# The gate projections of a hybrid attention trunk move out of the merge stage and wait in DRAM

## What is computed

```python
h = rms_norm(x, attn_norm_w[i])
proj = h @ w_in[i]
dq, dk, dv, cq, ckv, krope, xq, gates = jnp.split(proj, IN_SPLIT_POINTS, axis=-1)
...   # y_a: differential attention, 8 heads; y_b: latent attention (MLA), 8 heads; y_c: cross-attention, 4 heads
g_a, g_b, g_c = jnp.split(jax.nn.sigmoid(gates), N_BRANCHES, axis=-1)
x = x + (g_a * y_a + g_b * y_b + g_c * y_c) @ w_out[i]
h2 = rms_norm(x, ffn_norm_w[i])
f_gate, f_up = jnp.split(h2 @ w_gate_up[i], 2, axis=-1)
x = x + (jax.nn.silu(f_gate) * f_up) @ w_down[i]
```

## Time and profile before

| | |
|---|---|
| median of 3 runs | 2238.22 us (2237.4 to 2241.2) |
| profiled execution, its own time | 2232.99 us |
| its span, first to last instruction | 2231.2 us |
| granted TensorE clock, mean of the span | 0.959 (1 is 2.4 GHz) |
| PE busy | 2135.6 us (96%), 9581 matmuls |
| DVE, ACT, POOL busy | 1052.9, 867.8, 874.1 us |
| DMA | 191.29 MB, mean 86 GB/s |
| share of the chain that ended last | PE 79%, DVE 11%, ACT 6%, issue 4% |

### The profile page before, as it was taken

The page is one execution under the profiler, slowest core; times in us unless marked ns, Lnnn a source line. Parts: engine busy times, 40 slices in busy tenths (PEclk is TensorE's granted clock), DMA queues, the critical chain, the costliest instruction groups (busy, mean ns, idle before and its releaser), DMA issues.

```text
span 2231.2 us, 31130 instructions
## 1 busy us (share of the span) xinstructions
PE 2135.6 (96%) x9581; PEld 1712.5 (77%) x9581; DVE 1052.9 (47%) x1813; ACT 867.8 (39%) x1513; POOL 874.1 (39%) x402
## 2 busy tenths in 40 slices
PE   4999999989999999999989899999899999999998
PEld 3876777767888888888878677776688888888886
DVE  6458777773222433331144878777522234333212
ACT  4444545553222433223343454545522233322333
POOL 2433222213444354445643322222244444444564
PEclk7999989989999999999999999899799999999998
DMA  5322111113333333323343211112233333333333
GB/s 179 91 78 60 44 49 46 44 36 114 103 95 95 94 95 100 97 86 119 97 143 83 72 48 53 40 44 57 80 100 94 94 95 95 98 99 94 110 97 113
DMA packets 352101, 191.29 MB, mean 86 GB/s; under 512 B 22614, under 2 KB 348316, under 8 KB 351132
## 3 DMA queue, kind: packets, MB, share of 16 engines
q1 hardware_dynamic: 349582, 175.97, 27.6%
q10 hardware_dynamic: 2446, 14.44, 1.8%
HBM read 182.49 MB, written 7.86 MB: 85 GB/s over the span
## 4 chain that ended last, share of the span: by engine, by line
PE 79%; DVE 11%; ACT 6%; issue 4%; DVEq 0%; ACTq 0%; POOL 0%; POOLq 0%
PE proj L528 24%; PE proj L530 24%; PE proj L529 24%; DVE p_a L1244 3%; PE flip L578 2%; ACT p_a L879 2%; ACT k_hi_hi L858 1%; PE score L563 1%; DVE mid L1206 1%; DVE rot L1205 1%; DVE rot L1204 1%; PE att L511 1%; PE att L512 1%; PE att L510 1%; PE score L562 1%
## 5 line engine op out<-in xcount | busy, mean ns | idle before, releaser
L493 POOL TENSOR_TENSOR w_lo<-raw,w_hi 128x1024 fp32r<-128x1024 f32 x352 | 859.0, 2443 | 1336.4 <-ACT w_hi L858 1335.7
L528 PE MATMUL proj<-h_hi,w_hi 128*128 128x512 f32 (+1 forms) x1648 | 658.2, 399 | 5.9 <-ACT kvT L858 1.4
L530 PE MATMUL proj<-h_hi,w_lo 128*128 128x512 f32 (+1 forms) x1648 | 643.7, 391 | 0.0
L529 PE MATMUL proj<-h_lo,w_hi 128*128 128x512 f32 (+1 forms) x1648 | 643.6, 391 | 0.0
L858 ACT ACTIVATE w_hi<-raw 128x1024 fp32r<-128x1024 f32 x356 | 374.3, 1053 | 207.7 <-PE proj L530 79.7
L528 PEld LDWEIGHTS proj<-h_hi,w_hi 128*128 128x128 f32 (+1 forms) x1648 | 310.5, 188 | 79.0 <-issue 9.4
L529 PEld LDWEIGHTS proj<-h_lo,w_hi 128*128 128x128 f32 (+1 forms) x1648 | 310.6, 188 | 67.7 <-issue 4.4
L530 PEld LDWEIGHTS proj<-h_hi,w_lo 128*128 128x128 f32 (+1 forms) x1648 | 310.1, 188 | 66.0
L528 PE MATMUL proj<-hid_hi,w_hi 128*128 128x512 f32 x352 | 136.9, 389 | 0.0
L529 PE MATMUL proj<-hid_lo,w_hi 128*128 128x512 f32 x352 | 136.9, 389 | 0.0
L530 PE MATMUL proj<-hid_hi,w_lo 128*128 128x512 f32 x352 | 136.9, 389 | 0.0
(11 more groups left out here) (269 smaller groups left out, 3131.2 us busy)
## 6 DMA issues: line engine op xcount, KB each, us to landing
raw<-in_w_in SPq DMA_DIRECT2D x232, 256.0 KB, 3.0
raw<-in_w_gate_up SPq DMA_DIRECT2D x176, 256.0 KB, 3.0
raw<-in_w_down SPq DMA_DIRECT2D x96, 192.0 KB, 2.4
raw<-in_w_out SPq DMA_DIRECT2D x40, 256.0 KB, 2.8
raw<-in_w_mem_kv SPq DMA_DIRECT2D x32, 256.0 KB, 2.8
raw<-in_w_o_diff SPq DMA_DIRECT2D x32, 256.0 KB, 2.8
x_scratch<-xT ACTq DMA_DIRECT2D x2, 2048.0 KB, 9.1
raw<-in_w_o_mla SPq DMA_DIRECT2D x16, 256.0 KB, 2.7
```

Source lines behind the costliest of these rows:

```text
L493: g.tensor_tensor(w_lo[s][:, :], raw[s % 2][:, :], w_hi[s][:, :].bitcast(F32), ALU.subtract).then_inc(slot_lo.sem, 1)
L528: mm(o, hi[:, c:c + width], rh, start=start and k == 0, stop=False)
L529: mm(o, hi[:, c:c + width], rl, start=False, stop=False)
L530: ins = mm(o, lo[:, c:c + width], rh, start=False, stop=stop and k == n - 1)
```

## The change

- The 24 gate units of a layer leave stage E. Two of them run in A, two in a new stage Z (the old first slots of head 0), two in each of seven heads (slots 3 and 5 of six) and six in the last head, stage L. ACT copies each result from its bank into `gate_out` (`copy_gate`) and issues the store to `gate_scratch` in DRAM (`store_gate`). In E, ACT issues the loads into `gate_in`, three tiles for each output tile, two output tiles ahead (`load_gates`); the first two sets are loaded in the last head.
- Stage E has two slots per output tile. The three branch outputs go to the banks `score[0]`, `score[1]` and `score[2]`, MLA first, cross second, differential last. DVE scales the gates from SBUF in place, ACT applies the sigmoid in place.
- `k_lo` becomes `k1_lo` and `k2_lo`, of 128 rows each; the half without data is set to zero once per layer, and the score matmul takes all rows.
- k is projected into bank 1, and DVE forms k's low parts before it takes the maxima of the latent scores.
- The last head uses the same banks as the others for its scores, and takes 15 of the 16 splits of `outs`, in the order of `SPLIT`.
- The first two memory units go to `att` and `score[0]`.

The core of the diff:

```diff
-        k_lo = over_x("k_lo", 4)
+        k1_lo, k2_lo = over_x("k1_lo_zero", 4), over_x("k2_zero_lo", 5)
+        gate_out = [over_x(f"gate_out{b}", 6 + b, F32) for b in range(2)]
...
+        gate_in = here("gate_in", [P, 6, SEQ])
...
-        SLOTS = dict(C=(4, CROSS), A=(4, 1), B=(4, HEADS), E=(20, 2), F=(4, 2), G=(4, FT // 2), H=(8, 4))
+        SLOTS = dict(C=(4, CROSS), A=(6, 1), Z=(6, 1), B=(6, HEADS - 1), L=(6, 1), E=(8, 2), F=(4, 2), G=(4, FT // 2), H=(8, 4))
...
+            def gate(l, i):
+                return whole(w_in, l, C_GATE + i * P)
...
+                slot(l, "A", 0, 1, *gate(l, GATES_A))
+                slot(l, "A", 0, 2, *whole(w_in, l, C_CKV + P))
+                slot(l, "A", 0, 3, *gate(l, GATES_A + 1))
...
+                slot(l, "Z", 0, 0, *whole(w_in, l, C_DV))
+                slot(l, "Z", 0, 1, *reversed(whole(w_in, l, C_DQ)))
+                slot(l, "Z", 0, 2, *gate(l, GATES_Z))
+                slot(l, "Z", 0, 3, *reversed(latent(l, 0)))
+                slot(l, "Z", 0, 4, *whole(w_in, l, C_DK))
+                slot(l, "Z", 0, 5, *gate(l, GATES_Z + 1))
+                with sp.Fori(0, HEADS - 1) as h:
+                    slot(l, "B", h, 0, *whole(w_in, l, h * P + (C_DV + P)))
+                    slot(l, "B", h, 1, (0, tiles(mla_w_uq, l, 0, QT, h * 96 + 96, 96)), (QT * 96, tiles(mla_w_ukv, l, 0, KVT, h * P + P)))
+                    slot(l, "B", h, 2, *whole(w_in, l, h * P + (C_DQ + P)))
+                    slot(l, "B", h, 3, *whole(w_in, l, h * (2 * P) + (C_GATE + GATES_B * P)))
+                    slot(l, "B", h, 4, *whole(w_in, l, h * P + (C_DK + P)))
+                    slot(l, "B", h, 5, *whole(w_in, l, h * (2 * P) + (C_GATE + (GATES_B + 1) * P)))
+                for i in range(6):
+                    slot(l, "L", 0, i, *gate(l, GATES_L + i))
...
+                        slot(l, "E", jj, 2 * e, (0, tiles(w_o_mla, l, 0, 4, j)), (4 * P, tiles(w_o_cross, l, 0, 4, j)))
+                        slot(l, "E", jj, 2 * e + 1, *whole(w_o_diff, l, j))
...
-                            q, k, rows = ((q1, k1, slice(0, 64)), (q2, k2, slice(64, P)))[n - 1]
+                            q, k, k_lo = ((q1, k1, k1_lo), (q2, k2, k2_lo))[n - 1]
                             mm(o, q[:, cols], k[:, 0:(t + 1) * P], start=True, stop=False)
-                            mm(o, q[rows, cols], k_lo[rows, 0:(t + 1) * P], start=False, stop=False)
+                            mm(o, q[:, cols], k_lo[:, 0:(t + 1) * P], start=False, stop=False)
...
+                unit(l, "B", h, 0, 0, (gate_copied, gate_copied.at(l, "B", h)), KD, h_rhs, w=w(0)).then_inc(slot_done.sem, 1)
...
+                latent_units(l, "B", h, 1, w(1), n, (diff_ready, diff_ready.at(l, "B", n)), (v_copied, v_copied.at(l, "B", n, 1)))
...
+                unit(l, "B", h, 2, 1, (mla_ready, mla_ready.at(l, "B", n, 1)), KD, h_rhs, w=w(2)).then_inc(slot_done.sem, 1)
+                unit(l, "B", h, 3, 0, (kv_copied, kv_copied.at(l, "B", n, 1)), KD, h_rhs, w=w(3)).then_inc(slot_done.sem, 1)
...
+                unit(l, "B", h, 4, 1, (diff_ready, diff_ready.at(l, "B", n, 1)), 4, h_rhs, stop=False, w=w(4))
...
+                unit(l, "B", h, 4, 1, None, 4, lambda k: h_rhs(k + 4), first=4 * P, start=False, w=w(4)).then_inc(slot_done.sem, 1)
...
+                unit(l, "B", h, 5, 0, (gate_copied, gate_copied.at(l, "B", h, 1)), KD, h_rhs, w=w(5)).then_inc(slot_done.sem, 1)
+                latent_scores(l, n)
...
+            def last_head(l, h):
+
+                def gate(i, b, free):
+                    unit(l, "L", 0, i, b, free, KD, h_rhs).then_inc(slot_done.sem, 1)
+
+                gate(0, 0, (gate_copied, gate_copied.at(l, "L")))
+                pe.wait_ge(qk_split.sem, qk_split.at(l, "B", h, 2))
+                causal_scores(l, h, 1)
+                causal_flip(l, h, 0, 0)
+                gate(1, 1, (ssq_read, ssq_read.at(l, "B", h)))
+                causal_flip(l, h, 0, 1)
+                causal_scores(l, h, 2)
+                gate(2, 0, (gate_copied, gate_copied.at(l, "L", 0, 1)))
+                gate(3, 1, (gate_copied, gate_copied.at(l, "L", 0, 2)))
+                causal_attend(l, h, 0, mv_hi, mv_lo)
+                causal_flip(l, h, 1, 0)
+                gate(4, 0, (gate_copied, gate_copied.at(l, "L", 0, 3)))
+                causal_flip(l, h, 1, 1)
+                causal_attend(l, h, 1, v_hi, v_lo)
+                gate(5, 1, (gate_copied, gate_copied.at(l, "L", 0, 4)))
+                pe.wait_ge(a_squared.sem, a_squared.at(l, "B", h, 1))
+                pe.wait_ge(gate_copied.sem, gate_copied.at(l, "L", 0, 5))
+                pe.wait_ge(exp_done.sem, exp_done.at(l, "B", h + 1))
+                mm(proj[0][:, :], ones[:, :], a_sq[:, :], start=True, stop=True).then_inc(ssq_full.sem, 1)
 
...
-                project_mem(l, 0, 2, 0, (xq_copied, xq_copied.at(l, "C", 0, 1)))
-                project_mem(l, 0, 3, 1, (tile_ready, tile_ready.at(l, "C", 0, 1)))
+                project_mem(l, 0, 2, att, (att_read, att_read.at(l, "C")))
+                project_mem(l, 0, 3, score[0], (exp_done, exp_done.at(l, "C")))
...
+                unit(l, "Z", 0, 2, 1, (v_copied, v_copied.at(l, "B", 0, 1)), KD, h_rhs).then_inc(slot_done.sem, 1)
                 pe.wait_ge(pair_lo.sem, pair_lo.at(l, "A", 0, QT + KVT))
-                latent_units(l, 0, 2, (v_copied, v_copied.at(l, "B", 0, 1)), (diff_ready, diff_ready.at(l, "B", 0, 1)))
-                unit(l, "B", 0, 3, 0, (kv_copied, kv_copied.at(l, "B", 0, 1)), KD, h_rhs).then_inc(slot_done.sem, 1)
+                latent_units(l, "Z", 0, 3, ring("Z", 3), 0, (gate_copied, gate_copied.at(l, "Z", 0, 1)), (diff_ready, diff_ready.at(l, "B", 0, 1)))
...
+                        unit(l, "E", jj, 2 * e, score[0], (om_used, om_used.at(l, "E", jj, e)), 4,
                              lambda k: (outs_hi[:, 8 + k, :], outs_lo[:, 8 + k, :]), before=lambda k: split(8 + k)).then_inc(om_done.sem, 1)
-                        unit(l, "E", jj, s + 4, 1, (od_used, od_used.at(l, "E", jj, e + 1)), 4,
+                        unit(l, "E", jj, 2 * e, score[1], (oc_used, oc_used.at(l, "E", jj, e)), 4,
                              lambda k: (outs_hi[:, 12 + k, :], outs_lo[:, 12 + k, :]), first=4 * P,
                              before=lambda k: split(12 + k)).then_inc(slot_done.sem, 1)
...
+            def copy_gate(l, stage, step, s, b, k):
+
+                t = gate_stored[k % 2]
+                act.wait_ge(slot_done.sem, slot_done.at(l, stage, step, s + 1))
+                act.wait_ge(t.sem, t.at(l, stage, step, 16 * (k // 2)))
+                copy(gate_out[k % 2][:, :], proj[b][:, :]).then_inc(gate_copied.sem, 1)
+
+            def store_gate(l, stage, step, k, i):
+
+                act.wait_ge(gate_copied.sem, gate_copied.at(l, stage, step, k + 1))
+                act.dma_start(gate_scratch[bass.ds(i, 1), :, :].rearrange("a p n -> (a p) n"), gate_out[k % 2][:, :]).then_inc(gate_stored[k % 2].sem, 16)
+
+            def load_gates(l, jj, e):
+
+                for g in range(3):
+                    act.dma_start(gate_in[:, 3 * (e % 2) + g, :],
+                                  gate_scratch[bass.ds(jj * 4 + (e + g * KD), 1), :, :].rearrange("a p n -> (a p) n")).then_inc(gate_loaded[e % 2].sem, 16)
...
+                split_ahead(l, "B", h, 2, e)
+                split_ahead(l, "B", h, 3, e)
+                copy_gate(l, "B", h, 3, 0, 0)
+                split_ahead(l, "B", h, 4, e)
+                store_gate(l, "B", h, 0, h * 2 + GATES_B)
+                att_mla(l, h, h % 2 if isinstance(h, int) else e)
+                causal_high(l, h, 1, 0)
+                query_high(l, n)
+                split_ahead(l, "B", h, 5, e)
+                causal_high(l, h, 1, 1)
+                key_high(l, n)
+                copy_gate(l, "B", h, 5, 0, 1)
+                att_square(l, h)
+                store_gate(l, "B", h, 1, h * 2 + (GATES_B + 1))
+                values_high(l, n)
                 act.wait_ge(att_read.sem, att_read.at(l, "B", h))
...
+                        b, gates = e % 2, [gate_in[:, 3 * (e % 2) + g, :] for g in range(3)]
+                        ve.wait_ge(gate_loaded[b].sem, gate_loaded[b].at(l, "E", jj, 48 * (e // 2 + 1)))
+                        for g in (1, 2, 0):
+                            v.tensor_tensor(gates[g], gates[g], rstd_x[:, :], ALU.mult).then_inc(gate_scaled.sem, 1)
...
+                        v.tensor_tensor(mix[:, :], score[0][:, :], gates[1], ALU.mult).then_inc(om_used.sem, 1)
+                        ve.wait_ge(sig_ready.sem, sig_ready.at(l, "E", jj, 3 * e + 2))
+                        ve.wait_ge(slot_done.sem, slot_done.at(l, "E", jj, 2 * e + 1))
+                        v.tensor_tensor(gates[2], score[1][:, :], gates[2], ALU.mult).then_inc(oc_used.sem, 1)
+                        ve.wait_ge(oc_used.sem, oc_used.at(l, "E", jj, e + 1))
...
+                        v.tensor_tensor(gates[0], score[2][:, :], gates[0], ALU.mult).then_inc(od_used.sem, 1)
```

(20 more changed lines are left out.)

455 lines of the change are left out of this document (228 added, 227 removed).

## The result

The changed kernel takes 2247.5 us (median of 5 runs, 2246.6 to 2249.3) against 2238.2 before: a ratio of 1.0042, interval 1.0027 to 1.0056. It is slower by 0.4%, where I had forecast 2179. The experiments further down were timed on other chips, where the median of the kernel before was 2236.7, 2234.7 and 2234.2 us; each ratio is to the kernel before on the same chip, and between experiments on different chips the ratios compare better than the times. The profiled execution has a span of 2247.5 us, 16.3 longer than before, at a mean granted clock of 0.969.

A forecast was written before the change was run, and what follows sets the result against it. TensorE sets the time everywhere. Heads 19, last heads 32, latent stage 3 and memory units 5 make 59 us off the profiled 2233.0: 2174, plus 5.2 to the median, 2179 us; range 2135 to 2215.

The forecast's parts named there:

- The work of a head: Ordinary head without waits: 37.1 us of work, less 2.5 for padding, plus 10.9 for two gate units, 45.5.
- Wait (4): Ordinary head: k, projected into q's bank, waits for q's rope; 0.7 to 3 us, taken as 1.0.
- The clock term: Ordinary head: low clock costing 1.8 us in two heads of five, so +0.7 us per head.
- The rival with the right mechanism: Ordinary heads: w_lo holds q's rope, k's wait grows by 4.8, low clock 1.8; head 56.2, time 2262 us; chance 0.06.
- Wait (2): Ordinary head: mqT's wait for its rope grows from 0.64 to 1.9 us as the d2 scores end sooner.
- (5): Ordinary head: ACT squares the attention after key_high and the gate copy instead of before; 0.4 us.
- (1): Ordinary head: TensorE waits at the p_a flips for the chain over ACT and DVE; 0.8 us.
- The rival in which (2) does not come: Ordinary heads: w_lo misses mqT and q's rope; heads 46.7 us at full clock, time about 2140; chance 0.20.
- Wait (3): Ordinary head: the p_b wait, 0.68 us before, goes because a gate unit lies before its flips.
- The last head: Last head of each layer: 48.1 us with six gate units, 16 less a layer, 32 less in all.
- The gate stage: Two units or 10.9 us of TensorE per tile, no net change taken; at worst +3 us.
- Latent stage and head 0: Latent stage: q latents wait 1.4 us for a gate copy, k 2.4 for mqT's rope; net -3 us in all.

The follow-up runs named there:

- short w_lo: Changed kernel with GpSimd's low-part subtraction made on 128 of 1024 columns only, most of the weights' low part left out: 2083.9 us, ratio 0.9325.
- e5_last: Changed kernel with the last head's second low half ahead of eight outs_low on VectorE, and six gate loads at the head's end: 2234.0 us, ratio 0.9996.
- e1_bank: Changed kernel with k's projection back in bank 0 and the head's second gate projection in bank 1: 2158.5 us, ratio 0.9657.

## Why the prediction was wrong

**The work of a head was right.** 45.5 us for a head without waits; the kernel with short w_lo has 45.4. The price of the units and of the padding, nearly (1.1 us per set for 1.25), stands.

**Wait (4) is the step that failed.** I bounded k's wait for q's rotation by 0.7 and 3, and took 1.0, as if the second w_lo of a pair could cost the rotation only a little. It measured 3.2 in a usual head and 4.6 to 4.8 in the first two of each layer. I had looked for the hold on the rotation alone. The pair's second w_lo holds the combination first, and a third, behind the gate copy, holds the rotation: two holds of 2 us in one chain. The row that would have told me was at hand. The combination's 4.08 us in the earlier trace rows contain a hold of 1.9, as the 2.15 with the short w_lo shows, and a second w_lo directly behind the first had to lengthen it.

**The clock term failed with it.** I took 0.7 us a head, from two heads in five paying 1.8. Every usual head pays 3.4, in two stretches. In a head the two terms are 3.2 - 1.0 + 3.4 - 0.7 = 4.9 us too small, and three other waits were taken 0.9 too large. The heads came out at 54.8 for 50.3: in fourteen of them 63 us. With 2 x 6.4 for the last heads that is all of the 75 by which the sum of 2174 fell short of the profiled execution (2249.3).

**The rival with the right mechanism had 0.06.** It said that w_lo holds q's rotation, that k's wait grows and the clock falls, with a head of 56.2; the head is 54.8. That it comes so close is in part luck: it had 5.8 us for k's wait, which is 3.2, and 1.8 for the clock, which is 3.4. I argued it down because the trace of before had one hold per head on the path, and because units of 5.44 us would cover it. Neither is evidence on a chain with two more w_lo in it. The rule on which it stood, in the Trainium skill, "SBUF — State Buffer", section on the two separate sides (the pair of ports that VectorE and GpSimd share is locked for a whole instruction by whichever starts first), agrees with the rows here: 2.71 us for an add that began under w_lo, 0.69 for one that began 0.04 us before it.

**mqT, p_a, a_sq.** Wait (2) was forecast at 1.9 and measured 1.7, (5) at 0.4 and 0.3, (1) at 0.8 and 0.2. The rival in which (2) does not come falls with that. Wait (3), for p_b, went as forecast.

**The last head** was forecast at 48.1, with the second attention's wait at the lower end of its 2 to 3, and took 54.5. The step that failed is the second attention's wait, taken as 2 to 3: I counted one subtraction on VectorE, not the four outs_low (4.65 us) queued ahead of it. With that order changed it takes 48.0 and waits 2.2. The six gate loads took ScalarE 4.15 us, 0.69 each, where I had 0.33 from the earlier trace rows. TensorE waits 1.5 us ahead of the d2 scores in layer 1 and 0.4 in layer 2, and not at all in e5_last, where the loads come later; but in e1_bank, with the loads where they were, it is 0.2 in either, so how much of the 1.5 is theirs is open.

**The gate stage** runs without a gap, as said. Behind it 1.2 to 1.3 us per layer appear, a wait for `mix_lo` (the low part of the merged branches). **Latent stage and head 0:** the q latents wait 1.5 for the gate copy (forecast 1.4) and k 1.6 for mqT (2.4); what was missed is the 4.6 to 4.8 of the k projections in heads 0 and 1. **Memory units:** the 4.3 for qT went, and 4.7 of waiting for vT came at the flips of layer 2, so "some of it returns" was all of it there. The lower end of the heads' range, -57, is too small by its own terms: without waits (2) and (4) it is -19 less 14 x 2.9, -60.

**The padding** does what it says, and alone it is worth 3 us, because the waits behind it grow (some 9 if the late start of layer 2 in that trace, told at the end, is set aside; an estimate from one trace). The forecast had that for the second set only.

## What to carry to other kernels

Before you add work to a stage, list what each engine that shares a port with another will do there, and lay its instructions over the longest chain of the other, in time: six subtractions in place of four leave GpSimd busy for only 15.4 of 54.8 us, and cost VectorE 4 us in the one chain that counted. A busy time in a row is not a price; compare it with the same form elsewhere, since it may contain a hold already. When a product goes to another bank, ask who reads that bank last: another choice of banks for two of four products was worth 89 us here (86 by the ratios), and one more such choice, with the order of one copy and of the last head, 131 in all.
